# Two split weight buffers start at multiples of 256 bytes, and five small column tiles become one

## The reference: what is computed

```python
h = h + rmsnorm(mix, g[1])                                   # first model, 272 columns
ff = conv_ffn(rmsnorm(h, g[2]), ffn_w_up[l], ffn_conv[l], ffn_w_down[l])
h = h + rmsnorm(ff, g[3])
...
x = x + gate_m * y                                           # second model, 256 columns
h = rmsnorm_2(x, norm_ffn_g[layer]) * (1.0 + scale_f) + shift_f
x = x + gate_f * swiglu(h, ffn_w_gate[layer], ffn_w_up[layer], ffn_w_down[layer])
```

## The kernel before, in words

| tile | start | mod 256 |
|---|---|---|
| `work` | 37,792 | 160 |
| `c_row` | 46,912 | 64 |
| `raw` | 51,008 | 64 |
| `w_hi` | 83,776 | 64 |
| `w_lo` | 116,544 | 64 |
| first tile of a scope (`qfig`, `a_hi_up*`, `fox_heads`, `z_hi`) | 149,376 | 128 |
| `x_hi_a`, `x_lo_a`, `x_hi_up0`, `x_lo_up0` (rows of 1088 bytes) | | 128, each row 64 further |
| `x_hi_up1`, `x_lo_up1` (rows of 1088 bytes, read from column 14) | | 184, each row 64 further |
| `x_hi_e`, `x_lo_e`, `a_hi_up1`, `a_lo_up1` (rows of 1024 bytes) | | 128 |
| `z_hi` / `z_lo` (rows of 1032 bytes) | 149,376 / 157,632 | 128 / 192, each row 8 further |
| `a_hi_gu*`, `a_lo_gu*`, `mla_o_hi`, `mla_o_lo`, `xkv_hi`, `xkv_lo` (rows of 1024 bytes) | | 0 |
| `k_tok_a` / `coupling_level` | 214,784 / 217,024 | 0 / 192 |

## Time and profile before

### The profile page before, as it was taken

The page is one execution under the profiler, slowest core; times in us unless marked ns, Lnnn a source line. Parts: engine busy times, 40 slices in busy tenths (PEclk is TensorE's granted clock), DMA queues, the critical chain, the costliest instruction groups (busy, mean ns, idle before and its releaser), DMA issues. The chain is left out here.

```text
span 1529.3 us, 28962 instructions
## 1 busy us (share of the span) xinstructions
PE 1436.7 (94%) x11237; PEld 1380.1 (90%) x11237; DVE 1051.7 (69%) x1798; ACT 777.2 (51%) x1259; POOL 270.9 (18%) x360
## 2 busy tenths in 40 slices
PE   7998899999889998999979899989999999999997
PEld 7998789999888777999977799989999998899997
DVE  7773777877878726888777745357877657687653
ACT  6645554453476544454436555565343456544342
POOL 2001001220033400122001244002333100132210
PEclk9999989999999988999999999999999999999999
DMA  8533435559433203665953211136775635385451
GB/s 326 190 111 138 165 129 202 211 195 354 176 142 118 100 30 123 234 226 180 363 222 110 87 60 64 69 112 230 277 270 201 228 110 179 111 303 202 142 184 50
DMA packets 45700, 264.68 MB, mean 173 GB/s; under 512 B 8736, under 2 KB 10016, under 8 KB 20512
## 3 DMA queue, kind: packets, MB, share of 16 engines
q1 hardware_dynamic: 45600, 263.33, 47.6%
HBM read 262.26 MB, written 1.05 MB: 172 GB/s over the span
## 5 line engine op out<-in xcount | busy, mean ns | idle before, releaser
L257 DVE TENSOR_TENSOR w_lo<-raw,w_hi 128x2048 fp32r<-128x2048 f32 (+3 forms) x204 | 418.7, 2057 | 177.5 <-ACT w_hi L249 174.4
L249 ACT ACTIVATE w_hi<-raw 128x2048 fp32r<-128x2048 f32 (+3 forms) x221 | 380.1, 1725 | 83.0 <-PE bank L1233 43.4
L469 PE MATMUL bank<-z_hi,w_hi 128*128 128x258 f32 x704 | 199.9, 284 | 0.0
L471 PE MATMUL bank<-z_hi,w_lo 128*128 128x258 f32 x704 | 198.5, 282 | 0.0
L470 PE MATMUL bank<-z_lo,w_hi 128*128 128x258 f32 x704 | 198.2, 282 | 0.0
L470 PE MATMUL bank<-x_lo_up,w_hi 128*128 128x272 f32 (+1 forms) x656 | 188.1, 287 | 0.0
L469 PE MATMUL bank<-x_hi_up,w_hi 128*128 128x272 f32 (+1 forms) x656 | 187.2, 285 | 0.0
L471 PE MATMUL bank<-x_hi_up,w_lo 128*128 128x272 f32 (+1 forms) x656 | 186.6, 284 | 0.0
L470 PEld LDWEIGHTS bank<-z_lo,w_hi 128*128 128x128 f32 x704 | 133.4, 190 | 0.1
L471 PEld LDWEIGHTS bank<-z_hi,w_lo 128*128 128x128 f32 x704 | 133.0, 189 | 0.0
L469 PEld LDWEIGHTS bank<-z_hi,w_hi 128*128 128x128 f32 x704 | 132.8, 189 | 0.1
(11 more groups left out here) (516 smaller groups left out, 3924.2 us busy)
## 6 DMA issues: line engine op xcount, KB each, us to landing
raw<-w_gu SPq DMA_DIRECT2D x44, 1024.0 KB, 4.8
raw<-w_up SPq DMA_DIRECT2D x42, 1024.0 KB, 4.8
work<-w_ada SPq DMA_DIRECT2D x27, 1024.0 KB, 4.9
raw<-w_down SPq DMA_DIRECT2D x32, 704.0 KB, 5.4
raw<-w_dn SPq DMA_DIRECT2D x32, 704.0 KB, 4.1
mod_w_down<-w_ada SPq DMA_DIRECT2D x16, 1024.0 KB, 6.9
raw<-w_a_in SPq DMA_DIRECT2D x15, 1024.0 KB, 5.0
raw<-w_gdn_qkv SPq DMA_DIRECT2D x12, 1024.0 KB, 4.8
```

Source lines behind the costliest of these rows:

```text
L249: act.activation(w_hi[:, s, 0:blocks * P], raw[:, s, 0:blocks * P], ACT.Copy).then_inc(hi_split.sem, 1)
L257: dve.tensor_tensor(w_lo[:, s, 0:blocks * P], raw[:, s, 0:blocks * P], w_hi[:, s, 0:blocks * P].bitcast(F32), ALU.subtract).then_inc(lo_sp ...
L469: pe.matmul(o, w_hi[:, s, b], x_hi[:, xk, cols[0]:cols[1]], start=begin, stop=False)
L471: last = pe.matmul(o, w_lo[:, s, b], x_hi[:, xk, cols[0]:cols[1]], start=False, stop=end)
```

## The change

`sbuf` gets an alignment, and `w_hi` and `w_lo` are allocated with 256. `root_tok`, `mod_sum`, `eps_col`, `conv_last`, `gate_coef` and `head_norm_eps` become columns of one tile `small_columns`, which lies behind `w_lo`. `gate_tok` holds 104 of 128 columns in each half, and the copy into it is as much shorter. A helper `rows_on_lines` is defined and called nowhere. No instruction is added, removed or moved to another place in a queue.

```diff
+LINE = 256
...
-        def sbuf(c, name, shape, dt=F32):
-            return c.enter_context(nc.sbuf_tensor(name, shape, dt))
+        def sbuf(c, name, shape, dt=F32, align=32):
+            return c.enter_context(nc.sbuf_tensor(name, shape, dt, align_bytes=align))
+
+        def rows_on_lines(c, name, rows, width, lead=0):
+
+            pitch = -(-(lead + width) * 4 // LINE) * LINE // 4
+            return sbuf(c, name, [P, rows, pitch], F32R, LINE)[:, :, lead:lead + width]
...
-        root_tok = sbuf(ctx, "root_tok", [P, ROOT_COLS // SQUARE])
...
-        mod_sum = sbuf(ctx, "mod_sum", [P, 2, 2])
         c_row = sbuf(ctx, "c_row", [P, D])
         raw = sbuf(ctx, "raw", [P, SLOTS, ITEM])
-        w_hi = sbuf(ctx, "w_hi", [P, SLOTS, ITEM], F32R)
-        w_lo = sbuf(ctx, "w_lo", [P, SLOTS, ITEM], F32R)
+        w_hi = sbuf(ctx, "w_hi", [P, SLOTS, ITEM], F32R, LINE)
+        w_lo = sbuf(ctx, "w_lo", [P, SLOTS, ITEM], F32R, LINE)
+        small = sbuf(ctx, "small_columns", [P, 32])
+        root_tok, mod_sum = small[:, 0:9], small[:, 9:13].rearrange("p (l t) -> p l t", l=2)
+        eps_col, conv_last, gate_coef, norm_eps = small[:, 13:14], small[:, 14:20], small[:, 20:22], small[:, 22:23]
...
-        eps_col = sbuf(ctx, "eps_col", [P, 1])
-        conv_last = sbuf(ctx, "conv_last", [P, 6])
...
-                tok = sbuf(scope, "gate_tok", [P, 2, P])
-                coef = sbuf(scope, "gate_coef", [P, 2])
+                G, B, R, BR = 0, 32, 64, 96
+                tok = sbuf(scope, "gate_tok", [P, 2, BR + H])
+                coef = gate_coef
                 one_col = con("reset_hgrn", 0, 47)
-                norm_eps = sbuf(scope, "head_norm_eps", [P, 1])
...
-                        dve.tensor_copy(tok[:, :, :], bank[2][:, 0:2 * P].rearrange("p (x c) -> p x c",
-                                                                                   x=2)).then_inc(tok_made.sem, 1)
+                        turned_rows = bank[2][:, 0:2 * P].rearrange("p (x c) -> p x c", x=2)
+                        dve.tensor_copy(tok[:, :, :], turned_rows[:, :, 0:BR + H]).then_inc(tok_made.sem, 1)
```

More of the change, by code:

```diff
@@ L2159, in __init__ @@
                 late_q = sbuf(scope, "late_queries", [P, H, C])
-                G, B, R, BR = 0, 32, 64, 96
                 grown, beta, lean = (tok[:, :, i:i + H] for i in (G, B, R))
```

## The result

The changed kernel takes 1540.24 us (five runs, 1534.17 to 1542.42), the kernel before beside it 1530.45 us (five runs, 1528.38 to 1531.77). The ratio is 1.0053 with a 95% interval of 1.0036 to 1.0069: slower by half a per cent, where 1519.0 us was forecast. The profiled execution has a span of 1539.0 us against 1529.3 us.

The account below looks back on a forecast made before the run. The prediction took PE's matmul count times pace as the bound. Gains of 8.9 us on PE's path and 1.7 us in the mixers, 10.6 us together, took 1529.6 to 1519.0 us, with an 8-in-10 range of 1491 to 1537.

Parts of the forecast that it names:

- That pace times count is the time: In PE's matmul streams, hardly any idle time, so time is the matmul count times the start-to-start pace.
- The price of the weights' new place: Weight buffers from 64 to 0 mod 256: gain of 1.5 ns a matmul, 10.6 us together with mixers counted half.
- The 110 ns of the load-bound steps: 128-column matmuls bound by weight loads: 110 ns a step with the stationary tile at 0 or 192, so price 0.
- I give them nothing: The 1,056 matmuls with a_hi_gu (dn0, dn1), at 113.3 ns and within 4 ns of 110, were given no gain.
- slower, by the relative offset: Rival: operands' offset distance counts; dn0, dn1, mla_out lose 4.7 ns a matmul, 5.9 us, about 1536 us; chance 0.22.
- 258 and 272 columns don't move on average: Within the relative-offset rival: wide products' rows run through all offsets, so their mean pace stays.
- Two paces at unchanged addresses: GDN and MLA mixer streams: steady paces of 113.5 and 117.8 ns, addresses at most biasing which one a stream takes.
- `raw`, `work`, `c_row`, the small columns, `gate_tok` cost nothing: Moved tiles and merged columns taken as 0; 2 ns an instruction and 0.06 us for the gate_tok copy counted hidden.
- the loss that the prediction allowed for the moved `raw`: Rival: loads into raw at its new offset take 3% longer in 720 to 800 us, 2.4 us, 1532 us; chance 0.05.
- The Trainium skill's rule: TensorE's moving and weight reads use independent ports; by it the no-effect rival's sum is 0, 1529.6 us; chance 0.25.
- The range: Whole-kernel time for 8 in 10: 1491 to 1537 us, taking in both outer mechanisms nearly whole.

Follow-up runs that it names:

- e2: Changed kernel with w_hi and w_lo at 192 mod 256, scopes' tiles 256 bytes higher at the same offsets; executed once, 1538.7 us.
- e3: Changed kernel with w_hi and w_lo at 128 mod 256, scopes' tiles at the same offsets; executed once, 1541.0 us.
- e8: Changed kernel, weights left at 0, all activations of 256 columns moved to 192 mod 256; executed once, 1526.5 us.
- e4: Changed kernel with w_hi and w_lo at 96 mod 256, scopes' tiles at the same offsets; executed once, 1532.1 us.
- e1: Changed kernel with w_hi and w_lo back at 64 mod 256, small_columns ahead of them, all else left changed; ratio 0.9998 to the kernel before.
- The best version: e5 plus the 272-column rows of up0, HGRN2 and a_out starting on multiples of 256 bytes; 1523.73 us, ratio 0.9955 to the kernel before.
- e5: Changed kernel with weights back at 64 and the 256-column activations of down1 and GDN moved from 128 to 0 mod 256; ratio 0.9984 to the kernel before.

## Why the prediction was wrong

- **That pace times count is the time** was right: 8.8 of 9.7 us are pace.
- **The price of the weights' new place** is the step that failed: "I take a gain of 1.5 ns, a third of the way from 0 to 4.7". Both ends were the price of one operand's own offset. At 256 columns no such price shows; e2, e3 and e8 show that it is a property of the pair. In place of -1.5 ns on 5,136 matmuls the streams had +0.1 (`z`), +1.5 (`down1`), -0.5 (`up1`) and about 0 ns (272 columns). The 110 ns of the load-bound steps were true and told nothing of a 256-column stream.
- **"I give them nothing"** for `dn0` and `dn1` was the costly line: they had the fast pair (192), and a stream at the floor can only lose. It was 6.7 of the 9.7 us.
- **The rival "slower, by the relative offset"** had mechanism, place and sign. It priced the loss at 4.7 ns, the distance of the two paces that the trace showed, and the true one is 6.5: difference 0 has a pace of its own, 120.0, which no row of before held. It also said that `down1` and GDN would keep theirs; they lost 1.5 and 1.0 ns. Corrected, it gives 1530.5 + 8.0 + 1.7 = 1540.2. It had a chance of 0.22, too little: the earlier trace rows against the earlier trace rows could be read as a difference of 192 against 64 as well as an offset of 0 against 128, and nothing in the trace told these apart.
- **258 and 272 columns don't move on average**: nearly so here (+0.1, -0.5 and 0.0 ns), but partly by luck. The reason given was that their rows run through all offsets. Those of `z` don't: eight rows that step by 8 bytes cover 128 to 184 in `z_hi` and 192 to 248 in `z_lo`. e2 moved them by 1.3 ns, e4 the 272 columns by 0.8.
- **Two paces at unchanged addresses** The earlier trace rows was read rightly, and the sum made no use of it.
- **`raw`, `work`, `c_row`, the small columns, `gate_tok` cost nothing**: right by e1. Line 223 (now 230) took 1221 and 1219 ns in the earlier trace rows and takes 1222 and 1221 now; the copy into `gate_tok` took 365 ns where it had taken 414. The loads into `raw` are as they were: the median from issue to landing of `w_gu` is 4.8 us in both kernels, and a packet of 8 KB takes 309 ns at the median in both, so the loss that the prediction allowed for the moved `raw` isn't seen.
- **The Trainium skill's rule** (SBUF — State Buffer, "Who interferes with whom") of two independent read ports on TensorE: the two reads of this kernel are not independent in time, or 64 bytes in one operand's place couldn't change the pace from 113.3 to 120.0 ns. The measurement decides.
- **The range** ended at 1537 and the median is 1540.2: its upper end was about the rival's own time, with too small a price.

Open: what inside the chip the two reads meet on, what about a start picks one of the two paces at 192 or 64, how to choose it, and what a 258-column row wants. The best version was timed against the kernel before alone; that its gain comes from the rows is read from the paces (123.3 against 126.1 ns) and not from a run against e5.

## What to carry to other kernels

Alignment of a matmul's operands isn't a virtue of one buffer but a relation of two: measure the pace (start to start) for each pair of stationary and moving offsets, and before moving a buffer that all products share, list the streams that already have the best pace, since these pay. When a trace shows one operand's offset varied and the other's fixed, it can't tell "offset" from "difference", and the range has to hold both. A stream with two paces adds to the spread between runs of one program, by little where it is short: `mla_out` at 117.8 instead of 113.3 ns is 0.8 us. Most of the spread goes with the granted clock: the kernel before took 1525.1 us at 0.981 and 1534.6 us at 0.974. Before a gain of a few us is put down to a change, compare the clocks of the runs. And look at a stream stretch by stretch: an average of 115.5 ns was a mix of 113.3 and 117.8.

## What the runs showed of the hardware

- At 2.4 GHz, 256-column one-pass float32 matmuls, each with a new 128 x 128 stationary operand, run at one of a few paces (113.3, 117.8 or 120.0 ns at differences 192, 64 and 0; 118.7 and 116.7 seen at 128 and 32), whose mean holds to within 0.1 ns over hundreds of matmuls, while the columns alone take 106.7. At 1.2 GHz the excess is gone, at difference 0 too: in `dn0` of the changed kernel the distances at half clock are 213 to 214 ns once they are steady.
- The pace of these matmuls depends on the two addresses' difference modulo 256 bytes, in steps of 32 bytes or less. For 258 columns a move by 256 bytes changed it by 0.5 ns, so there this isn't the whole rule.
- The same program at the same addresses can run a stream at 113.3 or 117.8 ns (`mla_out`: 113.35 and 117.78 in two profiles), and in e5 the one gave way to the other across a wait of 2.78 us. The pace is settled at the start of an unbroken stretch and kept: in 107 stretches at difference 192 it never changed on the way.
